# Retention by 64-token blocks, outputs behind the next dense product, in a two-phase Hymba-style encoder step

## The reference, cut to what matters

```python
s = einsum('bqhd,bkhd->bhqk', q, k) * decay      # decay: gamma^(i-j), causal
inner = einsum('bhqk,bkhv->bqhv', s, v)
cross = einsum('bqhd,bhdv->bqhv', q, R) * q_dec  # gamma^(i+1)
R_new = gamma^L * R + einsum('bkhd,bkhv->bhdv', k * k_dec, v)
out = inner + cross
```

## Time and profile before

| | |
|---|---|
| median of 3 runs | 1840.75 us (1840.66 to 1842.19) |
| the profiled execution's own time | 1841.68 us |
| its span, first to last instruction | 1839.8 us |
| TensorE matmuls busy | 1793.3 us, 97%, 9636 instructions |
| VectorE busy | 1158.7 us, 63% |
| ScalarE busy | 578.5 us, 31% |
| DMA queue of SP | 58.6% of 16 engines' span |
| TensorE's mean granted clock | 0.991 of full speed |

### The profile page before, as it was taken

How to read it: one execution, slowest core, us unless ns; L and a number is a source line. 1 busy time by engine, 2 the same in 40 slices (tenths; PEclk the granted TensorE clock), 3 DMA queues, 4 the chain that set the end, 5 groups by cost and what they waited for, 6 DMA issues and landing times.

```text
span 1839.8 us, 31050 instructions
## 1 busy us (share of the span) xinstructions
PE 1793.3 (97%) x9636; PEld 1481.0 (80%) x9636; DVE 1158.7 (63%) x2588; ACT 578.5 (31%) x2032; POOL 115.7 (6%) x278
## 2 busy tenths in 40 slices
PE   5999999999999999999799999999999999999997
PEld 3787888888888888888678888888888888888886
DVE  3665566655666555665666766766666666666666
ACT  3321222212222212222334434434434344344342
POOL 1000000000000000010000000000000000000000
PEclk8999999999999999999899999999999999999999
DMA  9665555555555555554765565575565665655655
GB/s 374 201 169 172 134 147 148 136 137 139 127 151 147 125 142 134 138 141 133 199 172 157 155 191 147 155 187 143 165 180 147 172 170 147 182 163 146 191 141 143
DMA packets 488465, 296.64 MB, mean 161 GB/s; under 512 B 348626, under 2 KB 423570, under 8 KB 487396
## 3 DMA queue, kind: packets, MB, share of 16 engines
q1 hardware_dynamic: 488420, 296.08, 58.6%
HBM read 174.27 MB, written 121.71 MB: 161 GB/s over the span
## 4 chain that ended last, share of the span: by engine, by line
PE 92%; DVE 2%; issue 2%; DMA 2%; ACT 1%; SPq 1%; POOL 0%; POOLq 0%; DVEq 0%; ACTq 0%
PE bank L1305 80%; PE bank L1478 3%; PE bank L1501 2%; PE bank L1403 2%; PE bank L1389 2%; PE bank L1395 2%; PE bank L1401 2%; PE bank L1508 1%; DVE wl L321 1%; DMA stage<-in_w_out 1%; DMA xn_scratch<-xn 0%; PE bank L1458 0%; SPq L517 0%; DMA aqk_row<-aqk_scratch 0%; DMA xt<-in_x_prompt 0%
## 5 line engine op out<-in xcount | busy, mean ns | idle before, releaser
L1305 PE MATMUL bank<-wh,hh 128*128 128x512 f32 x1584 | 397.9, 393 | 5.9 <-DVE hh L1085 2.7
L1305 PE MATMUL bank<-wh,hl 128*128 128x512 f32 x1584 | 392.7, 390 | 0.0
L1305 PE MATMUL bank<-wl,hh 128*128 128x512 f32 x1584 | 391.8, 389 | 0.5 <-DVE wl L321 0.5
L1305 PEld LDWEIGHTS bank<-wh,hl 128*128 128x128 f32 x1584 | 297.8, 188 | 61.9
L1305 PEld LDWEIGHTS bank<-wl,hh 128*128 128x128 f32 x1584 | 297.2, 188 | 62.7 <-DVE wl L321 0.9
L1305 PEld LDWEIGHTS bank<-wh,hh 128*128 128x128 f32 x1584 | 292.9, 189 | 66.9 <-issue 7.3
L726 ACT ACTIVATE hf<-xn,tiny_a 128x128 f32<-128x128 f32 (+1 forms) x248 | 98.6, 480 | 373.8 <-DVE xn L919 373.8
L1228 DVE SCALAR_TENSOR_TENSOR a_gate<-a_gate,bank 128x128 f32<-128x128 f32 x132 | 29.1, 282 | 175.1 <-ACT a_gate L875 175.1
L1305 PE MATMUL bank<-wh,yh 128*128 128x512 f32 x528 | 132.1, 392 | 0.0
L1305 PE MATMUL bank<-wh,yl 128*128 128x512 f32 x528 | 130.8, 389 | 0.0
L1305 PE MATMUL bank<-wl,yh 128*128 128x512 f32 x528 | 130.8, 389 | 0.0
(11 more groups left out here) (167 smaller groups left out, 2434.5 us busy)
## 6 DMA issues: line engine op xcount, KB each, us to landing
xt<-in_x_prompt SPq DMA_DIRECT2D x64, 512.0 KB, 3.9
p_scratch<-p_in SPq DMA_DIRECT2D x264, 96.0 KB, 1.8
p_in<-p_scratch SPq DMA_DIRECT2D x66, 384.0 KB, 3.5
h_scratch<-hf SPq DMA_DIRECT2D x33, 512.0 KB, 2.9
hf<-h_scratch SPq DMA_DIRECT2D x33, 512.0 KB, 4.8
out<-xt SPq DMA_DIRECT2D x32, 512.0 KB, 4.5
xn_scratch<-xn SPq DMA_DIRECT2D x31, 512.0 KB, 2.9
xp<-xn_scratch SPq DMA_DIRECT2D x124, 128.0 KB, 3.1
```

The costliest lines, as they stand in the source:

```text
L1305: ins = mm(out, a[:, k, :], b[:, k, :], start=first and n == part[0] and k == chunks[0], stop=last and n == part[-1] and k == chunks[-1])
```

## The change: what it does

Retention is computed in blocks of 64 tokens, two (c = 0, 1) in each tile, with an intermediate state `state_mid` after the first.

- Scores: instead of a 128 x 128 matrix per head, two 64 x 64 ones. Block c uses the column half c of the array and writes partitions 64c to 64c + 63 of `qs_b`.
- Mask: on 4 x 64 columns instead of 4 x 128 (`decay` is halved; the tables for the decays now count within 64 tokens).
- State update: two products per head, of the row halves; block 0 goes to `upd_b`, block 1 to `ky_b`, which was only used by two tiles for a transposition.
- `state_mid` = gamma^64 state + block 0 (new, four VectorE operations after the rotation of q; signals `mid_done`); state = gamma^64 `state_mid` + block 1 (instead of gamma^128 state + update).
- Outputs (`weighted_values`): from `state` for block 0 and `state_mid` for block 1 in column halves, then from the masked scores in the quarters on the diagonal. They no longer stand right behind the state update but behind the dense product of k; in the last slot, which has no front, they stay.
- In the two tiles where TensorE transposes k into `ky_b`, it waits for the state first.

Some small tables are placed more tightly to make room. The diff without those:

```diff
--- before.py
+++ after.py
...
@@ -961,13 +962,23 @@
                 if back:
                     wait(dve, s_ready, t)
                     wait(dve, out_ready, t - 1)
-                    V.tensor_tensor(s_t[:, :], qs_b[:, :], decay[:, :], ALU.mult).then_inc(st_done, 1)
+                    V.tensor_tensor(s_t[:, 0:RH * HALF], qs_b[:, 0:RH * HALF], decay[:, :], ALU.mult).then_inc(st_done, 1)
                 if front:
                     wait(dve, za_ready, 4 * t + 1)
                     wait(dve, rope_loaded, 16 * (t + 1))
                     wait(dve, q_turned, t)
                     wait(dve, k_done, t)
                     rotate(t, za0, q_row, zq_read, q_mul, q_done)
+                if back:
+                    wait(dve, upd_ready, t)
+                    wait(dve, out_ready, t - 1)
+                    wait(dve, state_done, t - 1)
+                    st = state_s if static(i) and t - 1 == SAMPLE else state
+                    for h in range(RH):
+                        cols = slice(h * DK, (h + 1) * DK)
+                        last = V.scalar_tensor_tensor(state_mid[:, cols], st[:, cols], GAMMA[h] ** HALF, upd_b[:, cols],
+                                                      ALU.mult, ALU.add)
+                    last.then_inc(mid_done, 1)
                 if static(i) and t == SAMPLE:
                     for n in range(B_Q, B_GATE):
                         split_lo(dve, n)
@@ -985,11 +996,11 @@
 
                     wait(dve, gn_stat_done, t)
                     wait(dve, gn_var_done, t - 1)
-                    wait(dve, upd_ready, t)
-                    st = state_s if static(i) and t - 1 == SAMPLE else state
+                    wait(dve, mid_done, t)
                     for h in range(RH):
                         cols = slice(h * DK, (h + 1) * DK)
-                        last = V.scalar_tensor_tensor(st[:, cols], st[:, cols], GAMMA[h] ** P, upd_b[:, cols], ALU.mult, ALU.add)
+                        last = V.scalar_tensor_tensor(st[:, cols], state_mid[:, cols], GAMMA[h] ** HALF, ky_b[:, cols],
+                                                      ALU.mult, ALU.add)
                     last.then_inc(state_done, 1)
 
                     for h in range(RH):
@@ -1365,6 +1376,26 @@
                     wait(pe, ag_done, t)
                 dense(kg_b[:, 0:KV], *h_of(i, t), (wkvh, wkvl)).then_inc(zb_ready, 1)
 
+            def weighted_values(i, t):
+
+                wait(pe, gn_done, t - 1)
+                wait(pe, mid_done, t)
+                st = state_s if static(i) and t - 1 == SAMPLE else state
+                for h in range(RH):
+                    for c in range(2):
+                        rows, cols = slice(c * HALF, (c + 1) * HALF), slice(h * DK, (h + 1) * DK)
+                        if h == RH - 1 and c == 1:
+                            wait(pe, st_done, t)
+                        mm(out_b[rows, cols], q_t[:, h * DK + c * HALF:h * DK + (c + 1) * HALF],
+                           (st, state_mid)[c][:, cols], start=h == 0, stop=False, tile_position=(0, c * HALF))
+                for h in range(RH):
+                    for c in range(2):
+                        rows, cols = slice(c * HALF, (c + 1) * HALF), slice(h * DK, (h + 1) * DK)
+                        last = mm(out_b[rows, cols], s_t[rows, h * HALF:(h + 1) * HALF], v_row[rows, cols],
+                                  start=False, stop=h == RH - 1,
+                                  tile_position=(c * HALF, c * HALF))
+                last.then_inc(out_ready, 1)
+
             def slot(i, u):
                 t = 2 * i + u
                 front = not static(i) or t <= SAMPLE
@@ -1385,23 +1416,21 @@
                     wait(pe, qt_done, t)
                     wait(pe, kt_done, t)
                     for h in range(RH):
-                        c = slice(h * DK, (h + 1) * DK)
-                        last = mm(qs_b[:, c], k_t[:, c], q_t[:, c], start=True, stop=True)
+                        for c in range(2):
+                            tok = slice(h * DK + c * HALF, h * DK + (c + 1) * HALF)
+                            last = mm(qs_b[c * HALF:(c + 1) * HALF, h * HALF:(h + 1) * HALF], k_t[:, tok], q_t[:, tok],
+                                      start=True, stop=True, tile_position=(0, c * HALF))
                     last.then_inc(s_ready, 1)
                     wait(pe, state_done, t - 1)
                     wait(pe, v_done, t)
                     for h in range(RH):
-                        c = slice(h * DK, (h + 1) * DK)
-                        last = mm(upd_b[:, c], k_row[:, c], v_dec[:, c], start=True, stop=True)
+                        for c in range(2):
+                            rows, cols = slice(c * HALF, (c + 1) * HALF), slice(h * DK, (h + 1) * DK)
+                            last = mm((upd_b, ky_b)[c][:, cols], k_row[rows, cols], v_dec[rows, cols], start=True, stop=True,
+                                      tile_position=(c * HALF, 0))
                     last.then_inc(upd_ready, 1)
-                    wait(pe, gn_done, t - 1)
-                    st = state_s if static(i) and t - 1 == SAMPLE else state
-                    for h in range(RH):
-                        c = slice(h * DK, (h + 1) * DK)
-                        mm(out_b[:, c], q_t[:, c], st[:, c], start=True, stop=False)
-                        wait(pe, st_done, t)
-                        last = mm(out_b[:, c], s_t[:, c], v_row[:, c], start=False, stop=True)
-                    last.then_inc(out_ready, 1)
+                    if not front:
+                        weighted_values(i, t)
                 if static(i) and t == SAMPLE + 1:
 
...
@@ -1441,6 +1472,7 @@
                     dense(za1[:, :], h_hi, h_lo, group(3), part=early, last=False)
                     if pe_turns(i, t):
                         wait(pe, k_done, t + 1)
+                        wait(pe, state_done, t)
                         for h in range(RH):
                             c = slice(h * DK, (h + 1) * DK)
                             last = nc.tensor.transpose(ky_b[:, c], k_row[:, c], ident[:, :])
@@ -1575,12 +1607,13 @@
     ang = (row[:, None] * inv[None, :]).astype(np.float64)
     cos, sin = np.cos(ang), np.sin(ang)
     rope = np.concatenate([cos, -sin, sin], axis=1).astype(f).reshape(NT + 1, P, 192)
-    p = np.arange(P)
+    p = np.arange(P) % HALF
+    q = np.arange(HALF)
     g = np.array(GAMMA)
-    causal = (p[:, None] <= p[None, :]).astype(np.float64)
+    causal = (p[:, None] <= q[None, :]).astype(np.float64)
     decay = np.concatenate([causal * g[h] ** -(p[:, None] + 1.0) * DK ** -0.5 for h in range(RH)], axis=1).astype(f)
     qdec = np.concatenate([g[h] ** (p + 1.0) for h in range(RH)]).astype(f)[None, :]
```

More of the change, by code:

```diff
@@ L80, in build_program @@
         ident = sb("ident", [P, P])
-        small = sb("small", [P, 64])
+        small = sb("small", [P, 32])
         neg_half = small[:, 0:8]
@@ L111, in build_program @@
         state_s = sb("state_s", [P, COLS], F32, phase_a)
+        state_mid = sb("state_mid", [P, COLS], F32, phase_a)
         r_gate = sb("r_gate", [P, COLS], F32, phase_a)
         r_out = sb("r_out", [P, COLS], F32, phase_a)
-        decay = sb("decay", [P, COLS], F32, phase_a)
+        decay = sb("decay", [P, RH * HALF], F32, phase_a)
         qdec = sb("qdec", [P, COLS], F32, phase_a)
-        tiny_a = sb("tiny_a", [P, 176], F32, phase_a)
+        tiny_a = sb("tiny_a", [P, 96], F32, phase_a)
         vdec = tiny_a[:, 0:4]
@@ L119, in build_program @@
         gn_mv = tiny_a[:, 28:36].rearrange("p (h s) -> p h s", h=RH)
[L120 to L125, removed]
+        c_in = tiny_a[:, 4:20].rearrange("p (c k) -> p c k", c=2)
+        c_th = tiny_a[:, 20:36].rearrange("p (c k) -> p c k", c=2)
+        c_silu = tiny_a[:, 36:52].rearrange("p (k c) -> p k c", c=2)
+        g_col = tiny_a[:, 52:60]
+        h_scale = tiny_a[:, 60:76].rearrange("p (k c) -> p k c", c=2)
+        h_shift = tiny_a[:, 76:92].rearrange("p (k c) -> p k c", c=2)
         mod_rows = s_t
@@ L201, in build_program @@
             sem(n) for n in ("gn_stat_done", "gn_mv_done", "gn_var_done", "gn_rstd_done", "gn_done", "yr_done"))
-        state_out, wide_set = sem("state_out"), sem("wide_set")
+        state_out, wide_set, mid_done = sem("state_out"), sem("wide_set"), sem("mid_done")
         rows_cleared, h_front, hi_front, lo_front = sem("rows_cleared"), sem("h_front"), sem("hi_front"), sem("lo_front")
@@ L1577, in tables @@
     rope = np.concatenate([cos, -sin, sin], axis=1).astype(f).reshape(NT + 1, P, 192)
-    p = np.arange(P)
+    p = np.arange(P) % HALF
+    q = np.arange(HALF)
     g = np.array(GAMMA)
-    causal = (p[:, None] <= p[None, :]).astype(np.float64)
+    causal = (p[:, None] <= q[None, :]).astype(np.float64)
     decay = np.concatenate([causal * g[h] ** -(p[:, None] + 1.0) * DK ** -0.5 for h in range(RH)], axis=1).astype(f)
     qdec = np.concatenate([g[h] ** (p + 1.0) for h in range(RH)]).astype(f)[None, :]
```

(2 more changed lines are left out.)

## The result

The changed kernel takes 1930.76 us (median of 4 runs, 1930.5 to 1932.1) against 1840.7: 1.0487 of before, 95% interval 1.0473 to 1.05. The forecast was 1911 in a range of 1890 to 1942, slower with 96%. So sign and place were right and 20 of the 90 us were missing.

The account below looks back on a forecast made before the run. TensorE's instruction stream was taken as the bound; 32 tiles at 2.03 us more give 65, plus 2 for t = 30, 1.4 for the last tile and 1.5 for early ones: 70, so 1911 us, range 1890 to 1942.

Parts of the forecast that it names:

- TensorE's own stream: TensorE's work per loop tile without waits: 25.93 us, 0.58 us more than before.
- The prices of the changes of tiling: Six per tile: 0.15 us into 64-column tiles, 0.19 into row halves, 0.20 into the full array; 1.04 us together.
- The halved scores: Retention scores in two column halves side by side: eight steps in 0.45 us per tile instead of 0.89.
- The new wait on the keys' bank: TensorE waits 1.46 us per tile before the fourth dense product, until VectorE's rotation of k frees the bank.
- VectorE's tail: VectorE's work from bn_stats, 15.04 us into the tile, through k's rotation: 6.86 us, so the bank is free at 21.90.
- Rivals 1 and 4: Retention block: quarters not side by side, 1939 us, 14%; or column halves give back 0.45 us per tile, 1826, 2%.
- K's trip through DRAM: Store and load of k, third rival: slower than 8.09 us by over 0.2, TensorE waits at scores; 1943 us, 4%.
- The clock: TensorE's clock falling in the new waits was said to cost nothing that could be shown.
- the first tiles and the last slot: Outside the regular loop tiles: 1.5 us added for early tiles, 1.4 us for the last tile's longer block.

Follow-up runs that it names:

- e9: Changed kernel, buffers at old addresses, k rotated ahead of bn_stats, k's store and load moved first on SyncE's queue: 1867.42 us.
- e7: Kernel before, only its scores computed in two column halves side by side, each over all 128 columns of q: 1853.45 us.
- e4: Changed kernel with buffers back at old addresses and VectorE rotating k ahead of bn_stats: 1876.63 us.
- e10: Kernel before, 128-token products, outputs moved behind dense product of k, k rotated ahead of bn_stats, k's blocks first on SyncE's queue: 1847.23 us.
- e3: Changed kernel with one edit, VectorE rotates k ahead of bn_stats while the outputs are still being made: 1885.25 us.
- e2: Changed kernel with the table of small values back at 64 columns, so hh1, hl1, yh, yl lie where they lay before: 1916.15 us.
- e1: Kernel before with 32 instead of 64 columns in the table of small values, buffers after it 128 bytes lower: 1858.97 us.
- e11: Kernel before with 48 columns in the table of small values, buffers after it 64 bytes lower: 1844.98 us.

## Why the prediction was right, and where it was short

- TensorE's own stream: right. 25.93 forecast, 25.99 measured where nothing waits (e9). The prices of the changes of tiling, read from the attention phase, hold by themselves in e7 and together.
- The halved scores: right (0.46 for eight steps, 0.45 taken); the halves run side by side.
- The new wait on the keys' bank: right, 32 times. Counted as the prediction counts, from where the stream could have gone on, it is 1.56 us in the tile shown, against 1.46. bn_stats comes 0.08 later than forecast and VectorE's tail to TensorE's start is 7.02 us instead of 6.90.
- What a wait costs besides itself: left out. The first eight matmuls behind the wait take 562.68 to 564.64, 1.96 us instead of 1.81. So 0.15 x 32 = 5 us. The prediction compared the group of the earlier trace rows with one of the earlier trace rows that stands behind a change of tiling, and by how long each lasted (1.18 and 1.22). From start to start the group behind the wait took 1.03 us (902.05 to 903.08), the next one of the same form 0.95 (to 904.03): the refill could be read there.
- Rivals 1 and 4 fell, the first by the quarters, the fourth by the price of the changes of tiling. The quarters that share a bank ran side by side: one after the other their block would have been 1.03 + 0.89 us; it took 1.03. The Trainium skill, TensorEngine Tiling (Array Packing), Restrictions and Gotchas, says that different row tiles cannot access the same PSUM bank simultaneously; here the measurement differs, with disjoint partitions for the two halves.
- K's trip through DRAM did not bind in the changed kernel, but did as soon as the wait was removed (e4): it stood right behind.
- The clock: "costs nothing I can show" held for waits of 1.3 us. It did not for 2.77 and 3.18 us (e9, e10), where two groups ran partly at the lower of the two levels; behind e3's 2.76 us it did. What sets these apart stays open.
- The term that was missing: placement, 14.6 us in the changed kernel (e2) and 18 in the kernel before (e1). I had passed over the shorter table as a matter of room. With it, 1911 + 15 + 5 = 1931, but that it closes so well is partly luck. The scores of two neighbouring loop tiles of e2 start 27.6 to 27.7 us apart, not 27.38: the refill, 0.06 of TensorE's own stream and 0.04 of the wait, some 9 us in 32 tiles; and the first tiles and the last slot together took some 4 us less than I had set down for them.

The sum of what the change does, then: 21 us of TensorE's own work, 54 for VectorE's tail, the refills, t = 30 and the last slot (75 of e2 less 21), 15 placement. The version without tail and placement, 1867 us, still loses to the kernel before: blocks save 0.44 us of scores per tile and need six changes of tiling at 0.15 to 0.20, 0.64 us more in all. By the same prices (an estimate) the scores and the update alone would need three, 0.54. No experiment points to a version below 1841.

## What to carry to other kernels

On a stream that has no gap, moving an operation later removes nothing, and everything that the in-order consumer keeps behind it comes later too: look for what stands behind the result on its engine, and put first what frees the next buffer. Count changes of array tiling like instructions before splitting small products. And when a change shortens a table, compare the steps of products that the change does not touch: if they differ, addresses moved.

## What the runs showed of the hardware that I had not expected

- The start of the stationary operand within the partition: 128 bytes off its old place, up or down, makes a 128x512 matmul step at 232 instead of 227 ns (1.86 and 1.81 us per eight), 64 bytes off 1.83 us per eight. 3120 of the 6336 dense matmuls with 512 columns: 18 us, 1%. Where wkvh and wkvl lie 64 bytes lower (e11), the products of 256 columns with them went the other way, 0.90 instead of 0.96 us per eight.
- Behind a wait of 1.40 us, with the clock at 1.00, the first eight dense matmuls take 0.15 us more. Behind a change of tiling without a wait they take as much more (547.81 to 549.77).
- Waits of 2.77 us (e9) and 3.18 us (e10) were followed by the lower clock, one of 2.76 us (e3) was not.
- A change of tiling costs about 0.10 us to leave and 0.05 (64 columns) or 0.10 (128 columns) to fill with small products, in phase A as in the attention phase.
- Two quarters of the array on the diagonal, in different row halves, write different partitions of one bank side by side: sixteen passes in 0.89 us.
